# Nine SBUF blocks for expert weights in three turns, with four token tiles of h kept in DRAM meanwhile

## What is computed

```python
xn = rmsnorm(x, norm_mix)
h = x + token_mixer(xn, ...) @ w_out
hn = rmsnorm(h, norm_ffn)
# top-1 group of 4, then top-2 of its 8 experts
def expert_block(xb, e):                 # xb: rows of hn that chose expert e
    t = silu(xb @ w_eg[e]) * (xb @ w_eu[e])
    return t @ w_ed[e]
h = h + sum of the two picked experts' rows, each times its gate
y = rmsnorm(h, norm_final)
```

## Time and profile before

| What | Value |
|---|---|
| time, median of 3 runs | 1041.88 us (1039.87 to 1043.06) |
| profiled execution, its own time | 1040.4 us |
| its span, first to last instruction | 1038.6 us |
| mean granted TensorE clock | 0.991 |
| PE busy | 995.3 us (96%) |
| DVE busy | 564.6 us (54%) |
| DMA moved | 263.22 MB, mean 253 GB/s |

### The profile page before, as it was taken

The page is one execution under the profiler, slowest core; times in us unless marked ns, Lnnn a source line. Parts: engine busy times, 40 slices in busy tenths (PEclk is TensorE's granted clock), DMA queues, the critical chain, the costliest instruction groups (busy, mean ns, idle before and its releaser), DMA issues.

```text
span 1038.6 us, 33500 instructions
## 1 busy us (share of the span) xinstructions
PE 995.3 (96%) x14706; PEld 785.9 (76%) x14706; DVE 564.6 (54%) x1285; ACT 243.8 (23%) x531; POOL 105.2 (10%) x169
## 2 busy tenths in 40 slices
PE   7999999999999999999999999999999999999976
PEld 7785858585868686847787888888887787878842
DVE  2433535353544444426866666766756657566637
ACT  2352323232232323122011111111111110111125
POOL 0110101010101010101110111111111110101000
PEclk8999999999999999999999999999999999999989
DMA  9921010100010101656999999999999999999959
GB/s 313 337 95 42 1 42 0 40 0 40 0 40 0 40 0 41 243 205 237 370 362 419 421 420 422 420 425 418 424 418 419 423 414 426 414 418 420 388 190 390
DMA packets 55329, 263.22 MB, mean 253 GB/s; under 512 B 11385, under 2 KB 12985, under 8 KB 47067
## 3 DMA queue, kind: packets, MB, share of 16 engines
q1 hardware_dynamic: 44506, 235.19, 56.2%
q0 software_dynamic: 8192, 18.06, 4.6%
q10 hardware_dynamic: 2592, 9.44, 2.3%
HBM read 247.18 MB, written 27.19 MB: 264 GB/s over the span
## 4 chain that ended last, share of the span: by engine, by line
PE 78%; DMA 17%; DVE 3%; issue 1%; ACT 1%; SPq 0%; DVEq 0%; ACTq 0%
PE bank L1504 19%; PE bank L1790 18%; DMA arena<-in_w_ed 16%; PE bank L1622 11%; PE bank L1802 8%; PE bank L1556 6%; PE bank L1809 5%; PE bank L1490 1%; PE bank L1602 1%; DMA arena<-in_w_in 1%; PE bank L1874 1%; PE bank L1563 1%; PE bank L1619 1%; PE bank L1881 1%; PE bank L1883 1%
## 5 line engine op out<-in xcount | busy, mean ns | idle before, releaser
L1504 PE MATMUL bank<-xnT,arena 128*128 128x128 f32 x1728 | 201.4, 278 | 3.8 <-DMA arena<-in_w_in 2.5
L1504 PEld LDWEIGHTS bank<-xnT,arena 128*128 128x128 f32 x1728 | 197.1, 193 | 6.3 <-DVE late L1020 3.2
L1790 PEld LDWEIGHTS bank<-hnT,arena 128*64 128x64 f32 x4096 | 157.0, 137 | 10.3 <-issue 5.6
L1790 PE MATMUL bank<-hnT,arena 128*64 128x88 f32 x4096 | 160.1, 239 | 3.2 <-issue 1.6
L1622 PE MATMUL bank<-arena,mixT 128*128 128x512 f32 x256 | 111.7, 593 | 0.0
L1802 PE MATMUL bank<-arena,osq 128*32 128x384 f32 (+1 forms) x768 | 85.7, 487 | 8.8 <-DMA arena<-in_w_ed 8.8
L1622 PEld LDWEIGHTS bank<-arena,mixT 128*128 128x128 f32 x256 | 47.9, 190 | 57.2 <-issue 57.1
L1309 DVE TENSOR_SCALAR mixT<-mixT 128x352 f32<-128x352 f32 x32 | 14.1, 440 | 136.5 <-ACT mixT L874 136.5
L1790 PE MATMUL bank<-xnT,arena 128*64 128x88 f32 x2176 | 87.3, 239 | 0.8 <-issue 0.8
L1278 DVE STREAM_TRANSPOSE hnT<-xs 32x256 f32<-32x256 f32 x192 | 83.4, 435 | 7.5 <-DMA xs<-hn_rows,idx_i 1.3
L1790 PEld LDWEIGHTS bank<-xnT,arena 128*64 128x64 f32 x2176 | 85.0, 137 | 1.4 <-issue 1.3
(11 more groups left out here) (265 smaller groups left out, 1053.6 us busy)
## 6 DMA issues: line engine op xcount, KB each, us to landing
arena<-in_w_eu SPq DMA_DIRECT2D x32, 2048.0 KB, 9.1
arena<-in_w_ed SPq DMA_DIRECT2D x31, 2048.0 KB
arena<-in_w_eg SPq DMA_DIRECT2D x17, 2048.0 KB
work<-in_w_eg SPq DMA_DIRECT2D x15, 2048.0 KB
hn_rows<-hs ACTq DMA_DIRECT2D x18, 512.0 KB, 3.5
arena<-pick_rows SPq DMA_DIRECT2D x18, 512.0 KB, 9.9
arena<-in_w_in SPq DMA_DIRECT2D x4, 2048.0 KB
arena<-in_w_out SPq DMA_DIRECT2D x2, 2048.0 KB, 12.8
```

The costliest lines, as they stand in the source:

```text
L1504: last = mm(bank[n][:, m * P:(m + 1) * P], w[:, k, m * P:(m + 1) * P], xnT[:, k, :], start=k == 0, stop=k == KD - 1)
L1790: last = mm(out[q * SW:(q + 1) * SW, n * BLOCK:(n + 1) * BLOCK], w[:, k, m * P + q * SW:m * P + (q + 1) * SW], rowsT[b][:, k, :], start=k ...
```

## The change

A ninth block, `h_block`, is the place of token tiles 0 to 3 of `h_all`. When these four tiles are finished and normalized, SP stores them to a DRAM tensor `h_rows`, waits for that, and loads the gate weights of expert 2 in their place, still in the mixer. The nine blocks form three turns of three, and expert e uses turn e % 3, from the first expert to the last. Nine pieces now wait for no expert. After that a piece of expert e waits for the product of expert e - 3 that read its block. When the gate product of expert 29 is done, SP loads h back behind the last weights, and DVE's `combine` and PE's sums wait for that (`h_back`). The seven filler matmuls before PE's sums read tile 8 in place of tile 1. Because a block depends on e % 3 and the other buffers on e % 2, PE's loop body now holds six experts and runs five times, behind the same two experts of straight code. SP's loop holds three experts and runs nine times, with expert 30 and 31 behind it. ACT, DVE and POOL keep their loops.

```diff
@@ build @@
+    h_dram = nc.dram_tensor("h_rows", (P, KD * FF), F32, kind="Internal").ap()
...
-        blocks = [arena[:, n * EW:(n + 1) * EW] for n in range(6)] + [work[:, :], late[:, D:]]
+        h_all = sb("h_all", [P, TILES, D])
+        H_TILES = EW // D
+        h_block = h_all[:, 0:H_TILES, :].rearrange("p t d -> p (t d)")
+        blocks = [arena[:, n * EW:(n + 1) * EW] for n in range(6)] + [work[:, :], late[:, D:], h_block]
...
-        EVEN, ODD = (WORK, 4, 0), (1, 2, 3)
-        FIRST = ((0, 1, 2), (3, 5, LATE))
...
+        WORK, LATE, H = 6, 7, 8
+        MIXER_LOADS = [1, 1, 1, 1, 1, 1, 0, 0, 0]
+        BLOCKS_OF = ((0, 1, 2), (3, WORK, 4), (H, 5, LATE))
+        THIRDS = len(BLOCKS_OF)
...
-            def load_freed(t, b):
-
-                e = 2 * t + b
-                sp.wait_ge(s["pe_g"], e - 1)
-                load_piece(t, b, GATE)
-                sp.wait_ge(s["pe_u2"], 2 * (e - 1))
-                load_piece(t, b, UP)
-                sp.wait_ge(s["pe_d"], e - 1)
-                load_piece(t, b, DOWN)
-
+            def load_freed(e, turn):
+
+                freed = e - THIRDS + 1
+                sp.wait_ge(s["pe_g"], freed)
+                load_piece(e, turn, GATE)
+                sp.wait_ge(s["pe_u2"], 2 * freed)
+                load_piece(e, turn, UP)
+                sp.wait_ge(s["pe_d"], freed)
+                load_piece(e, turn, DOWN)
+
+            sp.wait_ge(s["hs_ready"], H_TILES)
+            sp.dma_start(h_dram, h_block).then_inc(s["h_kept"], 16)
+            sp.wait_ge(s["h_kept"], 16)
+            load_piece(2, 2, GATE)
...
-            with sp.Fori(2, NE // 2) as t:
-                for b in range(2):
-                    load_freed(t, b)
+            with sp.Fori(1, NE // THIRDS) as n:
+                for turn in range(THIRDS):
+                    load_freed(THIRDS * n + turn, turn)
+            for turn in range(NE % THIRDS):
+                load_freed(NE // THIRDS * THIRDS + turn, turn)
+            sp.wait_ge(s["pe_g"], NE - 2)
+            sp.dma_start(h_block, h_dram).then_inc(s["h_back"], 16)
...
+            dve.wait_ge(s["h_back"], 16)
             dve.wait_ge(s["g_fin_in"], 16)
             combine(0)
...
-            for b in range(2):
-                expert(0, b)
-            with pe.Fori(1, NE // 2) as t:
-                for b in range(2):
-                    expert(t, b)
+            for e in range(NE % (2 * THIRDS)):
+                expert(e, 0, e)
+            with pe.Fori(0, NE // (2 * THIRDS)) as n:
+                for at in range(2, 2 + 2 * THIRDS):
+                    expert(2 * THIRDS * n + at, 2 * n + at // THIRDS, at)
...
             for _ in range(SUMS_BUSY):
-                mm(bank[3][:, :], ident, h_all[:, 1, half_row(0)], start=True, stop=True)
+                mm(bank[3][:, :], ident, h_all[:, TILES - 1, half_row(0)], start=True, stop=True)
+            pe.wait_ge(s["h_back"], 16)
```

More of the change, by code:

```diff
@@ L230, in build, with weights @@
         GATE, UP, DOWN = range(3)
-        WORK, LATE = 6, 7
-        MIXER_LOADS = [1, 1, 1, 1, 1, 1, 0, 0]
-        EVEN, ODD = (WORK, 4, 0), (1, 2, 3)
-        FIRST = ((0, 1, 2), (3, 5, LATE))
[L236 to L249, removed]
+        WORK, LATE, H = 6, 7, 8
+        MIXER_LOADS = [1, 1, 1, 1, 1, 1, 0, 0, 0]
+        BLOCKS_OF = ((0, 1, 2), (3, WORK, 4), (H, 5, LATE))
+        THIRDS = len(BLOCKS_OF)
+        def weights(turn, kind):
+            return blocks[BLOCKS_OF[turn][kind]].rearrange("p (k n) -> p k n", k=KF if kind == DOWN else KD)
         cst = sb("cst", [P, N_CONST])
@@ L281, in build @@
         b_r_sb = sb("b_r_sb", [P, NL])
-        h_all = sb("h_all", [P, TILES, D])
         xs = sb("xs", [P, KD, P])
@@ L407, in build @@
             pe_xT pe_z pe_gate pe_qk pe_u pe_r pe_v pe_pool pe_kT pe_scores pe_kv pe_o pe_ones pe_wout pe_hT
[L408 removed]
+            pe_router pe_rank pe_idx first_idx_ready first_sel_ready first_rows_zero pads_zero h_kept h_back tile_out diag_ready pe_sums y_first_in lanes_skipped pe_half_out pe_own_T pe_first_rows pe_hist_T pe_small_T
             setup_dve setup_pool w_up_zero z_ready qk_ready ge_ready eb_ready enb_ready edec_ready u_ready er_ready v_ready kz_ready
@@ L492, in _, with load_piece @@
                     sp.dma_start(gla_sample[2 * p:2 * p + 2].rearrange("h k v -> (h k) v"), s_sample[:, p, :]).then_inc(s["states_stored"], 16)
-            def load_piece(t, b, kind):
-                e = 2 * t + b
+            def load_piece(e, turn, kind):
                 if kind == GATE:
@@ L502, in load_piece @@
                     src = w_ed[bass.ds(e * FF, FF), :].rearrange("(k p) n -> p k n", p=P)
-                sp.dma_start(weights(t, b, kind), src).then_inc(piece_in[place(t, b, kind)], 16)
-            def load_freed(t, b):
-                e = 2 * t + b
-                sp.wait_ge(s["pe_g"], e - 1)
-                load_piece(t, b, GATE)
-                sp.wait_ge(s["pe_u2"], 2 * (e - 1))
-                load_piece(t, b, UP)
-                sp.wait_ge(s["pe_d"], e - 1)
-                load_piece(t, b, DOWN)
+                sp.dma_start(weights(turn, kind), src).then_inc(piece_in[BLOCKS_OF[turn][kind]], 16)
+            def load_freed(e, turn):
[10 more added lines that the diff above has]
+            load_piece(2, 2, GATE)
             sp.wait_ge(s["pe_qk"], TILES)
@@ L521, in _ @@
             sp.wait_ge(s["pe_v"], TILES)
-            load_piece(0, 1, GATE)
+            load_piece(1, 1, GATE)
             sp.wait_ge(s["sA_ready"], TILES)
@@ L526, in _ @@
             sp.wait_ge(s["mixo_ready"], TILES)
-            load_piece(1, 0, GATE)
+            load_piece(1, 1, UP)
             sp.wait_ge(s["pe_half_out"], 1)
-            load_piece(1, 0, UP)
+            load_piece(1, 1, DOWN)
             sp.wait_ge(rows_in[0], 16)
@@ L532, in _ @@
             sp.wait_ge(s["pe_half_out"], 2)
-            load_piece(0, 1, UP)
+            load_piece(2, 2, UP)
+            sp.wait_ge(s["pe_router"], TILES)
+            sp.wait_ge(s["states_stored"], 16 * 2 * PAIRS)
+            load_piece(2, 2, DOWN)
             sp.wait_ge(s["pool_out_ready"], 2)
@@ L560, in _ @@
                         e = sp.value_load(steer[0:1, bass.ds(n + 1, 1)], min_val=0, max_val=NE - 1)
-                        sp.dma_start(weights(0, 0, GATE), w_eg[bass.ds(e * D, D), :].rearrange("(p k) n -> p k n", k=KD)).then_inc(s["x_w"], 16)
-                        sp.dma_start(weights(0, 0, UP), w_eu[bass.ds(e * D, D), :].rearrange("(p k) n -> p k n", k=KD)).then_inc(s["x_w"], 16)
-                        sp.dma_start(weights(0, 0, DOWN), w_ed[bass.ds(e * FF, FF), :].rearrange("(k p) n -> p k n", p=P)).then_inc(s["x_w"], 16)
+                        sp.dma_start(weights(0, GATE), w_eg[bass.ds(e * D, D), :].rearrange("(p k) n -> p k n", k=KD)).then_inc(s["x_w"], 16)
+                        sp.dma_start(weights(0, UP), w_eu[bass.ds(e * D, D), :].rearrange("(p k) n -> p k n", k=KD)).then_inc(s["x_w"], 16)
+                        sp.dma_start(weights(0, DOWN), w_ed[bass.ds(e * FF, FF), :].rearrange("(k p) n -> p k n", p=P)).then_inc(s["x_w"], 16)
                         wait_parted(sp, s["x_stored"], 16 * n + 16, s["parted"])
@@ L1820, in down, with expert @@
                 return last
-            def expert(t, b):
-                e = 2 * t + b
+            def expert(e, turns, at):
+                b = at % 2
                 first = isinstance(e, int) and e == 0
+                third = at % THIRDS
                 def loaded(kind):
-                    pe.wait_ge(piece_in[place(t, b, kind)], 16 * loads_until(t, b, kind))
+                    n = BLOCKS_OF[third][kind]
+                    pe.wait_ge(piece_in[n], 16 * (turns + MIXER_LOADS[n] + 1))
                 pe.wait_ge(s["eT_ready"], 1 if first else 2 * e + 2)
                 loaded(GATE)
-                up(bank[2 + b], weights(t, b, GATE), b, first=first).then_inc(s["pe_g"], 1)
+                up(bank[2 + b], weights(third, GATE), b, first=first).then_inc(s["pe_g"], 1)
                 loaded(UP)
@@ L1835, in expert @@
                 for half in range(2):
-                    up(bank[4 + half], weights(t, b, UP), b, HALVES[half]).then_inc(s["pe_u2"], 1)
+                    up(bank[4 + half], weights(third, UP), b, HALVES[half]).then_inc(s["pe_u2"], 1)
                 loaded(DOWN)
@@ L1839, in expert @@
                     pe.wait_ge(s["ye_ready"], YE_STEPS * e)
-                down(b, weights(t, b, DOWN), 2 * e + 1).then_inc(s["pe_d"], 1)
-            for b in range(2):
-                expert(0, b)
-            with pe.Fori(1, NE // 2) as t:
-                for b in range(2):
-                    expert(t, b)
+                down(b, weights(third, DOWN), 2 * e + 1).then_inc(s["pe_d"], 1)
+            for e in range(NE % (2 * THIRDS)):
[3 more added lines that the diff above has]
+                    expert(2 * THIRDS * n + at, 2 * n + at // THIRDS, at)
             pe.wait_ge(s["slots_ready"], 1)
@@ L1867, in _ @@
```

(9 more changed lines are left out.)

12 lines of the change are left out of this document (removed).

## The result

The changed kernel takes 1084.95 us (median of 4 runs, 1080.01 to 1089.02), the kernel before 1041.67 beside it (1039.87 to 1043.06): a ratio of 1.0411 [1.0388, 1.0435], 43 us slower. The profiled execution of the changed kernel has a span of 1084.5 us, 45.9 more than the earlier trace rows, and a mean granted clock of 0.974.

The account below looks back on a forecast made before the run. PE was taken to live on landed weights until 752 us, then wait for DMA. Less waiting (-14.4), streaming code (+28) and four jumps (+32) make +45.6 us on 1040.4, so 1086 us, range 1045 to 1116.

Parts of the forecast that it names:

- No waiting for weights: PE's experts behind expert 4: without waits for DMA's weights, expert 31 would start 14.4 us earlier.
- The body isn't held: PE's loop of six experts, 15 instruction packets: every expert's code is fetched again at every turn.
- Streaming: PE's experts 4 to 31: fetching code costs 1.0 us for each expert, 28 us in all.
- low bound of 0.6: Least cost in us of streaming code for each of PE's experts, with a third of the stops gone.
- Jumps: PE's loop branch: four jumps back to the body's start cost 8 us each, 32 us in all.
- high bound: Most that one jump of PE's loop could cost: 4.5 + 4 + 3.4 = 12 us.
- Sum: Start of expert 31 on PE: -14.4 + 28 + 32 = +45.6 us against before.
- DMA's side: Weight loads: one 2 MB load leaves the bound stretch (5.0 us), a gap closes (7.1 us), h's store and reload cost 0.
- The sum of 12.1 us: DMA's end in the expert part could come 5.0 + 7.1 us earlier, but hides nothing on the chain.
- The body is held: Rival on PE's loop code: nothing is refetched and DMA's side decides, 12.1 us earlier, 1028 us; chance 0.11.
- only the jumps cost: Rival on PE's loop: packets stream without stops, +3.6 to +17.6 us, 1044 to 1058 us; chance 0.08.
- Nothing to measure: Rival: body held, but row gathers on q0 queue longer and give back 12 us, 1038 to 1043 us; chance 0.03.

Follow-up runs that it names:

- experiment 3: PE's experts all written as straight code, without jumps: in the changed kernel 1054.01 us (1.0110), in the kernel before 1055.62 us (1.0133).
- experiment 1: The kernel before with only PE's loop over experts changed, to six experts and five turns, its eight blocks kept: 1084.09 us against 1042.55, 1.0389.

## Why the prediction was right, point by point

**No waiting for weights, -14.4 us.** Right: from expert 4 on no DMA of weights ends a wait of PE.

**The body isn't held.** Right, and it decides all. The page has 107 packets of q8. From 486 to 1040 us there are 89; I had put "about 75" behind expert 1, counting 2.5 for each expert. In straight code (experiment 3) there are 81 from 486 to 1000 us, 5 of them for experts 0 and 1: 76 behind expert 1, as counted. The changed kernel has 8 more, which makes two for each jump. I take them to be fetched and dropped there, which no run showed. I had called 15 far beyond the proven 5; in fact 9.5 and 10 aren't held either, and 5.8 is.

**Streaming, 1.0 us for each expert.** Nineteen intervals behind expert 4 have no jump beside them and a mean of 16.20 us, 0.94 over 15.26. In straight code it is 0.91. My low bound of 0.6, "a third of the stops gone", does not follow from the 4.6 us in four experts, which gives 0.8; only expert 2's 0.9 gives 0.6. The forecast does not rest on it.

**Jumps, 8 us each.** The four pairs of intervals at the jumps sum to 164.0 us. Less 8 x 15.26 and 8 x 0.94 this is 34.4 us, 8.6 each. All three parts of the working are in the rows: the first stop (5.2 to 5.7 us between weight loads, more than the 4.49 of the earlier trace rows at a low DMA load), the second (1.2 to 1.5, less than the 4 in my high bound), and the half clock, for instance 4.51 us for 57 rows that take 2.3 at full clock. Of the high bound's terms no row of before shows the 4 us for a second stop, and the changed kernel has the 1.2 to 1.5 in their place; the 3.4 us for the clock come from the 7 us of the earlier trace rows at 0.52, 7 x 0.48. By the same working the kernel of experiment 1 has 7.7 us for each jump, and the straight code of experiment 3 says 8.8, so the price is known to about 1 us.

**Sum.** -14.4 + 27 x 0.94 + 34.4 = 45.4; expert 31 starts at 1025.6 us for 979.87, 45.7 later, and the prediction had +45.6. The terms and the waits behind them were right. That the sum came so close is partly luck: streaming was 2.6 us too large (one expert too many and 0.06 us on each), the jumps 2.4 too small, and within a jump a longer first stop and a shorter second one than I had put offset each other.

**DMA's side.** The gap from 490 to 550 us is filled as said, and the store of h cost nothing: SP issues it at 247.34 us, when the DMA engines were nearly idle. Its reload is issued at 999.36 us and lands 13.0 us later; the first `combine` that waits for it starts at 1051.0 us, 39 us behind that. The sum of 12.1 us couldn't be seen in the changed kernel, as predicted, and where it can be seen it is 7.4, with the gap smaller there for PE's faster pace. DMA's rate is 402 GB/s in one turn of the loop and 394 from 554 to 1000 us; I had 390. One reading was slightly off: the 16.22 us that I called DMA's pace includes an interval at PE's own pace, since expert 17 still started without a wait; from expert 17 to 31 it is 16.29 us. The 14.4 us are a difference of two starts and don't depend on it.

**The rivals.** "The body is held" fell with q8's 107 packets, and "only the jumps cost" with the straight code, which has no jump and still loses 11 us. "Nothing to measure" needed a held body.

## What to carry to other kernels

Unrolling a loop further isn't free on an engine whose instructions are short: count its body in packets of 256 instructions (here 128 matmuls of 40 ns with their 128 weight loads from one stop to the next), and compare the time that one packet of work lasts with that of a fetch. Here a packet of gate and up lasted 5.1 us and the stops behind such packets 0.5 to 1.6 us, which makes 5.6 to 6.7 us for a fetch beside full weight queues (an estimate, which takes the next packet to be fetched while one is worked off). A body of up to 5.8 packets turned for nothing, one of 9.5 or more was fetched again at every turn. If a larger body can't be avoided, put its head on a packet's start (1073.69 us here for 1084.95) and give the hint for its back edge as well (1065.75); the hint by itself did nothing (1085.18).

## What the runs showed of the hardware that I had not expected

- The back-edge hint without an aligned head did nothing (1085.2 against 1085.0 us); with it it halved the first stop (2.5 to 2.6 us for 4.9 to 5.5) and, at three of four jumps, the clock stayed up (1073.7 to 1065.8 us).
- Each stop of 4.9 us or more at a jump was followed by half clock (a granted clock of 0.50): 3.5 to 11 us of it with narrow matmuls (stops up to 5.8 us), 29 to 31 us with wide ones (stops of 5.6 to 6.9 us). Of four stops of 2.5 to 2.6 us one was, for 3.4 us, and three were not.
- Among bodies that aren't held the larger one was not worse: ten packets with six jumps (1109 us) lost more than fifteen with four (1085 us), and straight code (1054 us) lost least, since it never jumps.
- Two strips of 64 weight columns take 77 ns, one of 128 columns with the same 88 moving columns 113 ns (float32).
- Not tried: bodies between 5.8 and 9.5 packets, and the nine blocks with a loop of two experts, which would need weight addresses that change from turn to turn.
